# Router of a mixture of experts on one core: GpSimd's clearing and last addition moved, fewer steps in group choice, one-hots and ranks, token rows in three transfers

## What is computed

```
x = x + gate1 * mix
h = rms_norm(x, norm2_w) * (1 + scale2) + shift2
pg = softmax(h @ wg)                 # 4 expert groups
g  = argmax(pg)                      # top-1 group, first one at a tie
pf = softmax(fine[g])                # 8 experts inside it (fine = h @ we, 32 columns)
top_p, top_i = top_k(pf, 2)
weight = pg[g] * top_p / sum(top_p)
y = sum over the two experts: weight * (silu(h @ w_gate) * (h @ w_up)) @ w_down
x = x + gate2 * y
```

## Time and profile before

| | us |
|---|---|
| timed runs, median of 3 | 1360.57 (1360.28 to 1360.92) |
| profiled execution | 1365.36 |
| its span | 1363.70 |
| PE busy | 1280.7 (94%) |
| VectorE busy | 722.3 (53%) |
| GpSimd busy | 304.6 (22%) |
| mean granted TensorE clock | 0.973 |

### The profile page before, as it was taken

One profiled execution on the slowest core, in us unless ns is written; L12 is line 12 of the kernel. 1 busy time (PEld: TensorE's weight loads), 2 busy tenths in 40 slices (PEclk: granted clock), 3 DMA queues, 4 the chain that ended last, 5 costly groups with the idle time before them and its releaser, 6 DMA issues. The chain is left out here.

```text
span 1363.7 us, 19640 instructions
## 1 busy us (share of the span) xinstructions
PE 1280.7 (94%) x6926; PEld 908.6 (67%) x6926; DVE 722.3 (53%) x1461; ACT 264.3 (19%) x580; POOL 304.6 (22%) x418
## 2 busy tenths in 40 slices
PE   7999999999999999998999999999999889988777
PEld 3787667788778787676777776778878633333226
DVE  1735588898878867310104557685667623221126
ACT  3201111222222344230212222200001300000001
POOL 0213424333423344122111115000001221111110
PEclk9999999999999999998999998999999889999997
DMA  9552243313322324556548320712248599999983
GB/s 371 184 112 87 79 153 124 124 63 128 132 72 102 124 70 146 198 171 194 173 141 337 119 85 17 265 48 93 72 162 352 202 363 418 419 418 419 420 318 132
DMA packets 71251, 259.30 MB, mean 190 GB/s; under 512 B 10981, under 2 KB 24581, under 8 KB 57178
## 3 DMA queue, kind: packets, MB, share of 16 engines
q1 hardware_dynamic: 54370, 221.99, 43.2%
q0 software_dynamic: 10112, 20.16, 4.4%
q10 hardware_dynamic: 6680, 15.96, 4.1%
HBM read 238.67 MB, written 27.44 MB: 195 GB/s over the span
## 5 line engine op out<-in xcount | busy, mean ns | idle before, releaser
L371 PE MATMUL psum<-arena 128*128 128x272 f32 x2408 | 568.9, 394 | 6.5 <-DVE arena L1393 1.9
L371 PEld LDWEIGHTS psum<-arena 128*128 128x128 f32 x2408 | 453.0, 190 | 118.4 <-issue 20.0
L393 POOL TENSOR_TENSOR arena<-arena 128x512 f32<-128x512 f32 x96 | 128.5, 1339 | 198.8 <-DMA arena<-in_weights 157.8
L3082 PE MATMUL psum<-arena 128*64 128x512 f32 x512 | 117.6, 607 | 16.9 <-DMA arena<-in_w_gu 14.5
L1537 PE MATMUL psum<-arena 128*128 128x272 f32 x512 | 124.1, 400 | 0.5 <-DVE arena L1702 0.5
L1537 PEld LDWEIGHTS psum<-arena 128*128 128x128 f32 x512 | 97.1, 192 | 26.8 <-DVE arena L1702 4.6
L2007 PE MATMUL psum<-arena 128*128 128x272 f32 x384 | 95.4, 402 | 3.0 <-PEq L213 3.0
L3082 PEld LDWEIGHTS psum<-arena 128*64 128x64 f32 x512 | 36.4, 139 | 87.7 <-issue 71.6
L2007 PEld LDWEIGHTS psum<-arena 128*128 128x128 f32 x384 | 72.7, 194 | 20.1 <-issue 5.4
L1702 DVE TENSOR_TENSOR arena<-arena,psum 128x272 f32<-128x272 f32 x16 | 7.0, 439 | 126.8 <-ACT arena L1633 126.8
L3173 DVE TENSOR_TENSOR arena<-arena,psum 128x256 f32<-128x256 f32 x16 | 6.8, 423 | 124.5 <-ACT arena L3164 124.5
(11 more groups left out here) (416 smaller groups left out, 1474.9 us busy)
## 6 DMA issues: line engine op xcount, KB each, us to landing
arena<-in_weights SPq DMA_DIRECT2D x153, 512.0 KB, 4.8
arena<-in_w_gu SPq DMA_DIRECT2D x64, 1024.0 KB, 23.7
arena<-in_w_down SPq DMA_DIRECT2D x32, 1024.0 KB, 25.3
arena<-in_weights ACTq DMA_DIRECT2D x16, 512.0 KB, 4.5
arena<-in_pages_k POOLq DMA_DIRECT2D x40, 128.0 KB, 3.4
arena<-in_x SPq DMA_DIRECT2D x2, 2176.0 KB, 11.9
y_rows<-arena SPq DMA_DIRECT2D x8, 544.0 KB, 16.6
arena<-in_pages_v SPq DMA_DIRECT2D x32, 128.0 KB, 3.1
```

Source lines behind the costliest of these rows:

```text
L371: mm = pe.matmul(out, lhsT=w[:, c * P:c * P + P], rhs=x[:, c, :], start=(c == 0 and not added), stop=(c == 3), skip_group_check=added or more)
L393: link(dve.tensor_tensor(sums[:, k], a, b, op))
L3082: mm = pe.matmul(psum[CAP * e:CAP * e + CAP, 2 + k, :].rearrange("p (o f) -> p o f", o=2), lhsT=xgT[:, k, lo:lo + CAP], rhs=wv[:, e, c2], ...
```

## The change

VectorE and GpSimd: GpSimd adds the squares of blocks up to 5 only; VectorE adds the two last ones, after its last scaling, and signals s_sqsum; GpSimd's clearing waits for that signal. TensorE sums the one accumulated buffer in one pass. The samples' scaling is done in two parts, the first during the last double block, straight into h's own columns, and their logits ride in the second product of each feature block (288 columns), so that the separate product goes.

```diff
+        if v == 3 and k == 2:
+            scaled_new(0, 6)
...
-    dve.tensor_tensor(xn11..., ALU.mult).then_inc(s_xn, 1)
+    scaled_new(6, DC)
+    dve.wait_ge(s_acc, DC - 3)
+    dve.wait_ge(s_sq11, DC - 1)
+    link(dve.tensor_tensor(acc11, acc11, sq11[:, 2, :], ALU.add))
+    dve.wait_ge(s_sq11, DC)
+    dve.tensor_tensor(acc11, acc11, sq11[:, 3, :], ALU.add).then_inc(s_sqsum, 1)
...
-    for c in range(1, DC - 1):
+    for c in range(1, DC - 2):
...
     pool.wait_ge(s_res, DC)
+    pool.wait_ge(s_sqsum, 1)
     pool.tensor_tensor(dshift, ...)
     pool.memset(xg_early, 0.0).then_inc(s_rows, 1)
     pool.wait_ge(s_rnew, 1)
+    pool.wait_ge(s_rl0, 1)
```

Choice of group and experts, ranks:

```diff
-    top_of(lg[:, :, NE:W_LG], g8, gi8)
-    link(dve.tensor_copy(gif, gi8[:, :, 0:1].bitcast(U32)))
-    link(dve.tensor_tensor(goh, iota, gif, ALU.is_equal))
-    link(dve.tensor_scalar(pen, goh, -1.0, 3e38, ALU.add, ALU.mult))
-    link(dve.tensor_tensor(masked, lg[:, :, 0:NE], pen, ALU.add))
+    link(dve.tensor_reduce(gtop, lg_group, AX, ALU.max))
+    link(dve.tensor_tensor(gis, lg_group, gtop, ALU.is_equal))
+    link(dve.scalar_tensor_tensor(gcode, iota, float(-NG), gis, ALU.add, ALU.mult))
+    link(dve.tensor_reduce(gfirst, gcode, AX, ALU.min))
+    link(dve.tensor_tensor(gnot, gcode, gfirst, ALU.not_equal))
+    link(dve.scalar_tensor_tensor(masked, gnot, -3e38, lg[:, :, 0:NE], ALU.mult, ALU.add))
...
-    for k in range(2):
-        last = dve.tensor_tensor(full[k], iota, eif[:, :, k:k + 1], ALU.is_equal)
+    link(dve.tensor_tensor(full2, iota, eif, ALU.is_equal))       # both one-hots, 320 columns
...
-    (four sums pre[:, 1..4] over earlier row blocks, signal s_pre)
...
-    pe.matmul(psum[:, 3, 0:4 * NE], lhsT=ones, rhs=pre[:, 0:4, :])  and three more with pre
+    for i in range(4):
+        pe.matmul(psum[:, 3, (i + 1) * NE:NR * NE], lhsT=ones, rhs=both[:, i:i + 1, :].to_broadcast([P, 4 - i, NE]))
+    (counts: five matmuls over both[:, i, :] instead of two)
+    turn_rows(4)                                                   # was before the ranks
...
-    (ranks: two scalar_tensor_tensor of 160 columns, slot one-hots in one instruction)
+    (ranks: one of 320 columns, slot one-hots in two, a signal each; TensorE's slot
+     matmuls wait for the half they need)
...
-    dve.tensor_scalar(tabf, psum[:, 7, 0:NP], float(NO_ROW), None, ALU.add)
-    dve.tensor_copy(tab_i, tabf).then_inc(s_tabi, 1)
+    dve.tensor_scalar(tab_i, psum[:, 7, 0:NP], float(NO_ROW), None, ALU.add).then_inc(s_tabi, 1)
```

Rows, weight blocks and signals:

```diff
-    if i == 4:
-        act.wait_ge(s_h2w[0], 16)
-    row = rows11[0:m, i % 4, :]
+    row = rows11[0:m, i, :]                                        # five buffers
...
-    act.dma_start(h2_rows[i * P:i * P + m, :], row)                # after each of the five
+    if i < 4 and i % 2:
+        act.dma_start(h2_rows[(i - 1) * P:(i + 1) * P, :], rows11[:, i - 1:i + 1, :])
+    if i == 4:
+        act.dma_start(h2_rows[SEQ:NT, :], row)
...
     if at == 12:
         sp.wait_ge(w_used, T_END)
+    if at == 14:
+        sp.wait_ge(s_row_sb, 4)
...
     with pool.Fori(0, n_rounds) as r:
+        pool.wait_ge(s_rows, 1)
         pool.wait_ge(s_idx, r + 1)
-        pool.wait_ge(s_rows, 1)
...
     dve.tensor_copy(rounds_i, mx[:, 0:1]).then_inc(s_slot, 1)
+    dve.sem_inc(s_act, 2)
+    dve.sem_inc(s_xsb, 1)
...
-    dve.sem_inc(s_act, 2)                                          # after the last-table work
     dve.sem_inc(s_yo, 1)
-    dve.sem_inc(s_xsb, 1)
```

More of the change, by code:

```diff
@@ L2813, in logits @@
                 def logits(c):
-                    for g in range(2):
-                        mm = pe.matmul(psum[64 * g:64 * g + 36, 0, 0:256], lhsT=router[:, c, :],
-                                       rhs=hT[:, c, 256 * g:256 * g + 256], start=(c == 0), stop=(c == DC - 1))
-                    return mm
[L2819 to L2824, removed]
+                    for g, n in ((0, 256), (1, 256 + NEW)):
+                        mm = pe.matmul(psum[64 * g:64 * g + 36, 0, 0:n], lhsT=router[:, c, :],
+                                       rhs=hT[:, c, 256 * g:256 * g + n], start=(c == 0), stop=(c == DC - 1))
+                    return mm
                 pe.wait_ge(s_res, 7)
+                pe.wait_ge(s_xn, 1)
                 for c in range(DC - 1):
                     pe.wait_ge(s_xs, c + 1)
+                    if c == 6:
+                        pe.wait_ge(s_xn, 2)
                     logits(c)
[L2830 to L2833, removed]
+                pe.wait_ge(s_sqsum, 1)
+                for q in range(4):
+                    pe.matmul(psum[32 * q:32 * q + 32, 1, 0:P], lhsT=const("ones")[:, 0:32],
+                              rhs=acc11[:, q * P:q * P + P], start=True, stop=True)
+                pe.matmul(psum[:, 2, 0:NEW], lhsT=const("ones"), rhs=acc11[:, SEQ:NT],
+                          start=True, stop=True).then_inc(s_ss11, 1)
                 pe.wait_ge(s_xs7, 1)
                 logits(DC - 1).then_inc(s_rl0, 1)
[L2836 to L2840, removed]
                 pe.wait_ge(s_std11, 2)
@@ L2932, in _ @@
-                link(dve.tensor_tensor(pre[:, 2, :], both[:, 0, :], both[:, 1, :], ALU.add))
-                link(dve.tensor_tensor(pre[:, 3, :], pre[:, 2, :], both[:, 2, :], ALU.add))
-                dve.tensor_tensor(pre[:, 4, :], pre[:, 3, :], both[:, 3, :], ALU.add).then_inc(s_pre, 1)
-                values = const("row_values").rearrange("p (a b) -> p a b", b=NR)
-                for k in range(2):
-                    dve.tensor_tensor(pick[:, 0, NR * k:NR * k + NR], full[k],
-                                      bc(values[:, k, :].unsqueeze(2), NR, NE), ALU.mult)
@@ L2939, in _ @@
-                dve.wait_ge(s_rank, 1)
-                for k in range(2):
-                    last = dve.scalar_tensor_tensor(tmp32[:, k], psum[:, 3, 0:NR * NE].rearrange(
-                        "p (i e) -> p i e", e=NE), -1.0, full[k], ALU.add, ALU.mult)
-                link(last)
-                link(dve.tensor_reduce(rank, tmp32.rearrange("p k i e -> p (k i) e"), AX, ALU.add))
+                lg_group = lg[:, :, NE:NE + NG]
+                link(dve.tensor_reduce(gtop, lg_group, AX, ALU.max))
@@ new lines, in _ @@
+                for i in range(NR):
+                    last = dve.max(e8[:, i, :], masked[:, i, :])
+                link(last)
+                for i in range(NR):
+                    last = dve.max_index(ei8[:, i, :].bitcast(U32), e8[:, i, :], masked[:, i, :])
+                link(last)
+                link(dve.tensor_copy(eif, ei8[:, :, 0:2].bitcast(U32)))
+                link(dve.tensor_tensor(full2.rearrange("p (k i) e -> p k i e", k=2),
+                                       iota[:, 0:NE].unsqueeze(1).unsqueeze(1).to_broadcast([P, 2, NR, NE]),
+                                       eif.rearrange("p i k -> p k i").unsqueeze(3).to_broadcast([P, 2, NR, NE]),
+                                       ALU.is_equal))
@@ L3115, in slots @@
                 def slots(n, o, first=False):
-                    if o == 0:
-                        pe.wait_ge(s_onehot, n)
-                    elif first:
+                    if o and first:
                         pe.wait_ge(s_pickw, 1)
```

148 lines of the change are left out of this document (70 added, 78 removed).

## The result

| | before | after |
|---|---|---|
| timed side by side, median of 11 runs | 1362.48 | 1366.9 (1363.26 to 1369.46) |
| ratio to the kernel before | | 1.0027 [1.0014, 1.0039] |
| profiled execution | 1365.36 | 1368.19 |
| its span | 1363.7 | 1366.5 |

The change makes the kernel slower by 0.27%, some 3.7 us (1.9 to 5.3). On the 1360.57 shown ahead of the prediction that makes 1364.2; forecast were 1361.1 and a range up to 1363.5. Single executions of one kernel lie 4 to 12 us apart here, so the small questions are answered by marks inside the traces, counted from **t0**, the start of VectorE's last 512-column residual step (1066.79 before, 1065.99 after). Up to there the two kernels do the same but for small shifts (the first part of the samples' scaling). Counted from t0, the gather goes out at 21.02 before and 24.14 after: 3.1 later.

What follows compares the result with a forecast made beforehand. The expert-weight stream, begun after the first token-row gather, was taken to bound the kernel. Gather +0.9 and hole -0.4 made +0.5 on 1360.57, so 1361.1 us; range 1358.0 to 1363.5.

Steps and rivals of the forecast that it cites:

- What bounds the kernel: Whole kernel: weight stream starts after the first gather; a microsecond off the gather is one off the end.
- Blocks 14 and 15: SyncE's held weight blocks run beside row writes; sharing by halves, landing at 1087.5, gather 0.9 later.
- rival C: Row writes: weights take two thirds of the engines, gather 1087.8 to 1090.4, time 1363.2; chance 0.21.
- Samples' rows issued late: Row writes: samples' transposes end after the counts, issue at 1083.25, 0.7 later; the gather waits for this landing.
- Clearing and last addition: Router front, VectorE and GpSimd: contention removed, two additions moved to VectorE; line 2901 starts 0.8 earlier.
- rows 5: Profile rows for the router front: beside GpSimd, line 2737 takes 1.33 instead of 0.18, line 2761 2.30.
- Group choice: VectorE's expert-group selection: fewer, smaller steps, with 0.4 added for contention with GpSimd; gain 0.5.
- One-hots, ranks: Ranks to slot table: prefix sums go to TensorE; slot matmuls start 1.6 earlier, index up to 2.9 earlier.
- Signals: VectorE's signals before its last table work: TensorE 0.4 nearer to the gather, freeing slots 0.4 sooner.
- the hole: DMA gap 1114 to 1116, block waiting for TensorE to free a slot; shrinks by about 0.4 (0 to 0.6).
- B: Row writes: rows not slowed by the held weights, -0.4 - 0.4, time 1359.8; chance 0.23.
- D: Before the gather: index stays the last wait, samples' rows early, -2.9 - 0.4, time 1357.3; chance 0.11.

Runs made afterwards that it cites:

- The old kernel with the wait: Kernel before plus SyncE's wait holding weight blocks 14 and 15 until the fourth row block is copied; ratio to before 1.0011 [0.9998, 1.0024].
- the best version: Changed kernel without SyncE's wait for copied rows before blocks 14 and 15, samples' rows transposed before the ranks; ratio 0.9986, again 0.9987.
- the kernel after without the wait: Changed kernel with only SyncE's wait of blocks 14 and 15 for the copied rows taken out; ratio to before 1.0001 [0.9989, 1.0014].
- the front alone: Kernel before with only GpSimd's clearing and the last addition moved and the sums in one pass; one run 1362.81, before 1362.67.

## Why the prediction went wrong, point by point

*What bounds the kernel* held: gather, weight stream, end. After the first transposes (28.32 after, 25.75 before) the end follows by 272.2 and 271.2; but two executions of one kernel differ in this figure by 1.2 (269.8 and 271.0), so a microsecond of the gather is one of the end only to about that much. The old kernel with the wait shows it: gather 1.1 later, end 0.4. The figure goes with TensorE's clock in the first experts. From the first transposes on the granted clock stays at 0.50 for 6.8 us where the end follows by 269.8 (the best version, second run), for 7.9 where by 271.0 (its first run), for 8.5 before (271.2), for 9.2 after (272.2) and for 9.2 in the kernel after without the wait (272.2); all fourteen traces lie within 0.5 of this line, a microsecond for a microsecond. So of the 3.6 at the end 2.6 are the later transposes and 1.0 goes with the clock, and the kernel without the wait, its transposes 0.8 earlier than before, ends no earlier. No run changed this clock alone; it is a relation, not a shown cause.

*The step that failed is "Blocks 14 and 15": "I take halves".* From 1080 on the rows got a third, the value that the text had given rival C. The forecast put the gather at 21.9 from t0 (1088.7 on the clock of the trace before), rival C at 23.6; it was issued at 24.14, 2.2 later than forecast. From the trace after: by 1080.0 the rows had moved 0.88 + 0.17 MB of their 2.23, and 1.93 MB of weights were still to come. The remaining 1.18 take 5.8 us at half of 0.41 MB/us, which puts the last byte at 1085.8. At a third they have moved 0.97 when the weights are through at 1087.1, and then, with the engines to themselves, end at 1087.6. So the wrong share is 1.8 us, an estimate from these rates.

The last byte was at 1088.28, 0.7 later still: from 1087 to 1088 the engines moved only 217 GB/s, though hardly any weights were left. A third term was not in the sum at all: when the blocks' reads began beside the writes, 0.34 MB were moved in two microseconds (1078 to 1080), 1.2 us lost. It was made good by rows whose first bytes moved 1.0 sooner than I had put them (9.84 from t0, not 10.86). My 1.7 from issue to first bytes was read where the last weights were still in the engines; with these empty, as in the kernel after, it is 0.9. The queue rows for it, from 1075 to 1078 and then from 1078 to 1079 (packets, MB, share of the engines):

```profile
q10 hardware_dynamic: 215, 0.88, 73.6%
...
q1 hardware_dynamic: 15, 0.12, 127.7%
q10 hardware_dynamic: 57, 0.17, 46.8%
```

The rule of the Trainium skill (DMA: Bandwidth & Descriptors, Queues, rings and completion order) that I had weighed, turns by packets, fits the nearly equal counts (65 and 61, 72 and 65); that it is the size of the pieces which sets the share was not tested, since no run changed it, and one overlap below doesn't go by it. I chose the middle between two rows of a software queue, whose gathers have pauses of their own; I had no row of two full hardware queues side by side, and the sizes of the pieces were the only thing that spoke on it.

*Samples' rows issued late*: forecast 16.46 from t0 and 0.7 later than before, measured 17.53. The sign was right; it was of no weight beside the bytes, as the early transposes with the wait show.

*Clearing and last addition*: forecast 0.8 for line 2901, measured 1.07 (6.99 from t0 before, 5.92 after), of which the front alone gives 0.54; the other half comes with the samples' scaling and their separate product. The clearing in its new place (1069.62 for 1.81) cost nothing that shows in this sum. That rows 5 "agree on both kinds" is more than they show: the addition beside line 2737 is of the kind named, but line 2761, with one SBUF input, was slowed to 2.30 beside a clearing that only writes (0.49 without it), and that the quoted rule doesn't tell.

*Group choice*: forecast a gain of 0.5 with the 0.4 of contention taken off; measured 0.43 (second maximum at 10.10 before, 8.60 after, less the 1.07). The contention is 0.43, shown by itself.

*One-hots, ranks*: the ranks end 1.8 earlier (14.66 to 12.88). Then the gain is lost: counts 1.81 where 1.35 was forecast and the samples' transposes 1.89 for 1.05, since the clock fell to 1.2 GHz within the counts. These 1.3 us are most of what put the slot matmuls at 16.38 in place of 15.26, and at 2.67 they were above the bound of 2.4. The forecast had taken the clock from the row of before, in which it fell at 17.2; the text gave the slot matmuls a range for it and nothing in front of them. With the clock up and the samples' transposes moved ahead, the index comes at 17.19, the near end of the forecast (17.1 to 18.2), and VectorE's one-hots let the slot matmuls start at 15.1: VectorE's steps were counted rightly.

*Signals*: forecast 0.4 on TensorE and 0.4 off the hole. The signal is worth 0.2. For the hole, the windows of before from 1112 to 1118 (that of 1114 is in the earlier trace rows)

```profile
1112.00:1114.00 2.00, 2.00 (x12) 0.62 (x10) 0.00 (x0) 0.00 (x0) 0.00 (x0) 1.00 0.93 356
...
1116.00:1118.00 2.00, 2.00 (x11) 0.70 (x12) 1.23 (x1) 0.00 (x0) 0.00 (x0) 1.00 1.01 377
```

lack (68 + 211 + 47) x 2 / 424 = 1.5 us of data against 424 GB/s, those of after from 1114 to 1120, with its row of 1114 above,

```profile
1116.00:1118.00 2.00, 2.00 (x14) 1.00 (x10) 0.42 (x1) 0.39 (x1) 0.00 (x0) 1.00 1.00 365
1118.00:1120.00 2.00, 2.00 (x11) 0.77 (x12) 1.22 (x1) 0.00 (x0) 0.00 (x0) 1.00 0.99 414
```

(129 + 59 + 10) x 2 / 424 = 0.9: 0.6 less, with a later gather. A term of that size is not to be told from the spread of 1.2 above.

*Chances*: C had 0.21 and came true in mechanism and place, and its gather, 23.6 from t0, was 0.5 too early. B is false with the wait (5.28, not 2.9). D's picture, the index last, is reached only without the wait and with early transposes, and there 1.8 of its 2.9 us for the gather. C's time, 1363.2, lies 1.0 below the measured 1364.2: besides the half microsecond of the gather it had no term for the clock, with which 1.0 of the traces' 3.6 us went.

## What to carry to other kernels

Before you hold back a prefetch "until the small writes are out", count the bytes that then stand before the landing you wait for, and try the sum with shares by pieces and not only with halves: here the queue with pieces half as large got half as many bytes. 2 MB of weights that nobody waited for delayed the gather behind 2 MB of rows by 3.4 us; a landing is early when nothing else is in the engines, and issuing it earlier does not help while something is. And count a saved step on TensorE at both clock levels: the same forty slot matmuls took 1.66 or 2.67, and the same kernel showed both.

## What had not been expected of the hardware

- **A pause when large reads start.** In the kernel after 49 GB/s from 1079 to 1080 between 393 and 391 GB/s, with a DMA share of 1.75 in the microsecond before it (the 15 packets of weights above, 127.7%). The kernel with early transposes shows it too, in the windows where the blocks start:

```profile
1073.00:1074.00 1.00, 1.00 (x12) 0.99 (x10) 0.32 (x1) 0.51 (x2) 0.00 (x0) 1.00 1.01 393
1074.00:1075.00 1.00, 1.00 (x10) 0.92 (x9) 0.29 (x1) 0.70 (x1) 0.00 (x0) 1.00 1.17 148
1075.00:1076.00 1.00, 1.00 (x9) 0.86 (x8) 0.69 (x2) 0.89 (x1) 0.00 (x0) 1.00 0.50 172
```

  The start of the reads is slow by itself. The first 15 packets of weights took 1.4 us each in the kernel after (127.7% of 16 engines' microsecond), where later ones take 0.31. When block 16 starts, no rows are being written and hardly anything else moves, and the same trace shows the first 11 packets at 0.85 each (1095.0 to 1095.5) and the rate down again, with 360 GB/s in the microsecond that follows:

```profile
1095.00:1096.00 1.00, 1.00 (x6) 0.88 (x5) 0.00 (x0) 0.00 (x0) 0.73 (x1) 0.50 0.74 131
```

  What is particular to the place beside the writes is that the row pieces stand still as well, from 1078.6 to 1080.2. Why the first packets take so long is open: no run changed the size of the pieces or the place that is read.
- **Rows issued into running weights did not share with them.** With five writes the first row transfer was issued at 1075.09 and its first piece moved at 1078.24, 3.2 later, when the weights were nearly through; in between (1075.1 to 1078.2) only they moved:

```profile
q1 hardware_dynamic: 150, 1.10, 98.7%
```

  With the engines empty it took 0.9 (kernel after), in the versions without the wait 1.7. So the third is what two queues show that are both under way, not a rule for every overlap; here the one in front had it all. The cause is open.
- **The clock falls at another moment in another execution of one kernel**, at 14.6 or 17.1 from t0, with the same instructions in front of it: in the one during TensorE's wait of 0.80 ahead of the slot matmuls, in the other during the wait of 1.78 behind them. With the waits filled it kept 2.4 GHz until 21.4.
- **GpSimd needs about a microsecond from its last wait to the issue of an indirect DMA**: index to gather is 1.03 to 1.04 in every trace where the index is last, landing to gather 1.2 to 1.3 where the landing is.
